# Computing the expert gates between the activation products of a PEER layer

## What is computed

```python
def peer(xn, w_q, sub_keys, u, v):
    ...
    best_s, best_pos = lax.top_k(cand_s, PEER_TOPK)
    idx = jnp.take_along_axis(cand_i, best_pos, axis=-1)
    gate = jax.nn.softmax(best_s, axis=-1)
    ...
        act = jnp.einsum("cd,ced->ce", xc, uc).astype(jnp.float32)
        hid = (jax.nn.gelu(act, approximate=False) * gc).astype(xc.dtype)
        return jnp.einsum("ce,ced->cd", hid, v[ic])
```

## Time and profile before

| | us |
|---|---|
| median of 3 runs (1920.65 to 1923.58) | 1921.12 |
| the profiled execution | 1920.95 |
| its span, from first to last instruction | 1919.2 |
| PE busy | 1662.7 (87%) |
| PE weight loads | 1331.6 (69%) |
| DVE busy | 1301.7 (68%) |
| ACT busy | 706.9 (37%) |
| POOL busy | 451.9 (24%) |

### The profile page before, as it was taken

How to read it: one execution, slowest core, us unless ns; L and a number is a source line. 1 busy time by engine, 2 the same in 40 slices (tenths; PEclk the granted TensorE clock), 3 DMA queues, 4 the chain that set the end, 5 groups by cost and what they waited for, 6 DMA issues and landing times. The chain is left out here.

```text
span 1919.2 us, 25753 instructions
## 1 busy us (share of the span) xinstructions
PE 1662.7 (87%) x9316; PEld 1331.6 (69%) x9316; DVE 1301.7 (68%) x1434; ACT 706.9 (37%) x929; POOL 451.9 (24%) x257
## 2 busy tenths in 40 slices
PE   6986998788887877788989959999996679999997
PEld 6855555444444536677678959999995568888886
DVE  3345887777777734855216996666659988888887
ACT  4514776666666624243233422222237720000000
POOL 5602111111111105532135840000019930000000
PEclk9996899999999988797999989999999989999999
DMA  8416999999999985421412533555550015555554
GB/s 282 144 50 259 367 397 397 396 396 396 396 396 397 397 324 149 173 89 47 158 37 111 176 131 132 185 187 178 192 176 0 0 66 197 195 188 189 194 196 142
DMA packets 142119, 406.90 MB, mean 212 GB/s; under 512 B 11128, under 2 KB 14328, under 8 KB 125560
## 3 DMA queue, kind: packets, MB, share of 16 engines
q1 hardware_dynamic: 136408, 395.77, 57.3%
q10 hardware_dynamic: 5664, 10.49, 1.5%
HBM read 396.80 MB, written 10.35 MB: 212 GB/s over the span
## 5 line engine op out<-in xcount | busy, mean ns | idle before, releaser
L1983 DVE TENSOR_TENSOR ring_rest<-ring,w_lead 128x2048 fp32r<-128x2048 f32 x128 | 291.7, 2320 | 86.1 <-ACT w_lead L1110 86.0
L1110 ACT ACTIVATE w_lead<-ring 128x2048 fp32r<-128x2048 f32 x128 | 237.8, 1904 | 92.2 <-DMA ring<-in_w_gate 42.9
L2187 DVE TENSOR_TENSOR rest<-raw,lead 128x2048 fp32r<-128x2048 f32 x112 | 256.8, 2293 | 3.9
L2179 DVE CAST lead<-raw 128x2048 fp32r<-128x2048 f32 x112 | 137.4, 1227 | 153.3 <-PE bank L1710 98.9
L711 POOL TENSOR_TENSOR ring_rest<-ring,half_lead 128x2048 fp32r<-128x2048 f32 (+1 forms) x38 | 172.5, 4554 | 233.6 <-ACT half_lead L705 233.5
L1513 PE MATMUL bank<-w_lead,x_two 128*128 128x512 f32 x512 | 154.6, 438 | 56.2 <-ACT w_lead L1110 49.1
L616 ACT ACTIVATE xhat<-h 128x1024 f32<-128x1024 f32 x6 | 6.3, 1056 | 457.0 <-DVE h L2254 360.7
L1513 PE MATMUL bank<-ring_rest,x_two 128*128 128x512 f32 x512 | 149.0, 419 | 29.3 <-DVE ring_rest L1983 29.1
L1513 PEld LDWEIGHTS bank<-w_lead,x_two 128*128 128x128 f32 x512 | 93.7, 200 | 115.8 <-ACT w_lead L1110 87.3
L1766 PE MATMUL bank<-lead,hid_hi 128*128 128x512 f32 x512 | 158.8, 392 | 5.5 <-DVE hid_lo L2230 5.5
L1766 PE MATMUL bank<-rest,hid_hi 128*128 128x512 f32 x512 | 158.6, 391 | 0.0
(11 more groups left out here) (317 smaller groups left out, 2710.5 us busy)
## 6 DMA issues: line engine op xcount, KB each, us to landing
ring<-in_w_gate SPq DMA_DIRECT2D x32, 2048.0 KB, 19.7
ring<-in_w_up SPq DMA_DIRECT2D x32, 2048.0 KB, 22.6
ring<-in_w_down SPq DMA_DIRECT2D x32, 2048.0 KB, 20.2
raw<-in_u SPq DMA_DIRECT2D x64, 1024.0 KB, 4.9
raw<-in_v SPq DMA_DIRECT2D x64, 1024.0 KB, 4.9
ring<-in_w_in SPq DMA_DIRECT2D x14, 2048.0 KB, 11.8
ring<-in_w_out SPq DMA_DIRECT2D x4, 2048.0 KB, 7.8
y_sorted<-y_blk ACTq DMA_DIRECT2D x64, 128.0 KB, 5.4
```

Of the source, the lines that this page charges most:

```text
L1110: act.activation(w_lead[half][:, :, :], ring8(slot)[:, 4 * half:4 * half + 4, :], ACT.Copy).then_inc(w_lead_ready, 1)
L1983: dve.tensor_tensor(ring_rest8(slot)[:, part, :], ring8(slot)[:, part, :], w_lead[half][:, :, :].bitcast(F32), ALU.subtract).then_inc(w_re ...
L2179: return dve.tensor_copy(dst, src)
L2187: dve.tensor_tensor(rest[slot][:, :], raw[slot][:, :], lead[b][:, :].bitcast(F32), ALU.subtract).then_inc(rest_ready, 1)
```

## The change

The gates' groups move from their own stage into the second part of the activation products. `ROUTING` goes from 16 to 24, so POOL and ACT split 24 chunks (POOL 25) before PE waits for the routing. From chunk 24 on the code of all engines is unrolled. `groups_in(n)` spreads the 64 groups over the 38 chunks 25 to 62: 26 of these have two groups, 12 have one. PE does a chunk's first half, the groups of that chunk, and then its second half. ACT makes `lead` for all chunks of `u`, its Gelu and its one-hots; DVE makes only `rest` there. DVE no longer multiplies a whole column in one go: where a token's gates come before the chunk's activation, DVE has copied the gates into `A` (`gate_columns`, the copy), ACT takes Gelu in place in PSUM, and `mix_columns` multiplies the two; where the activation came first, `gate_columns` multiplies as before. Activation products use three banks instead of two, gates three instead of four. POOL multiplies straight by `bestT` and no longer copies. Because `lead` is in use all the time, two of the three one-hot buffers lie on the residual `h`; SP saves `h` to DRAM before the stage and loads it back when all groups are done, and loads the last gain there too. Before the output products, the second chunk of `v` is split behind the last `mix_columns`. A semaphore is dropped elsewhere, its wait going to another with the same meaning.

```diff
-ROUTING = 16
+ROUTING = 24
+POOL_RESTS = ROUTING + 1
 PEER_CHUNKS = NKEYS // CJ
 HK = PEER_HEADS * TOPK
 GT = 4
 GROUPS = T // GT
-HOTS = 4
-VECTOR_HOTS = 1
-SCALAR_HOTS = HOTS - VECTOR_HOTS
+HOTS = 3
+FIRST_MIXED = POOL_RESTS
+LAST_MIXED = PEER_CHUNKS - 2
+def groups_through(n):
+    spans = LAST_MIXED - FIRST_MIXED + 1
+    return min(max(n - FIRST_MIXED + 1, 0), spans) * GROUPS // spans
+def groups_in(n):
+    return range(groups_through(n - 1), groups_through(n))
+def vector_makes_both(g):
+    return g % 4 == 0
+SCALAR_TURN = {g: k for k, g in enumerate(g for g in range(GROUPS) if not vector_makes_both(g))}
...
+        bestT = at("bestT", [P, T], WORK + 5120)
+        ijT = at("ijT", [P, 2, T], WORK + 6144)
+        hot = [at(f"hot{b}", [P, 2, GT, NKEYS], (H_AT, H_AT + 4096, WORK)[b]) for b in range(HOTS)]
+        h_kept = nc.dram_tensor("h_kept", (P, NT * D), F32, kind="Internal").ap()
...
+        ACT_BANK = [4, 5, 6]
+        GATE_BANK = [7, 0, 1]
+        ROUTE_BANK = [0, 1]
...
+            sp.dma_start(h_kept, h[:, :, :].rearrange("p t d -> p (t d)")).then_inc(h_saved, 16)
...
+            sp.wait_ge(gates_done, GROUPS)
+            sp.wait_ge(h_saved, 16)
+            sp.dma_start(h[:, :, :].rearrange("p t d -> p (t d)"), h_kept).then_inc(final_in, 16)
+            sp.wait_ge(chunk_used, PEER_CHUNKS)
+            sp.dma_start(gain_f[:, :], dram["norm_f_g"].broadcast_to([P, D])).then_inc(final_in, 16)
...
+            for n in range(ROUTING, POOL_RESTS):
+                pool_rest(n, n)
...
+            for g in range(GROUPS):
+                weighted = hot[g % HOTS][:, 1, :, :]
                 pool.wait_ge(hot_ready, g + 1)
...
-                pool.tensor_tensor(hot[b][:, 1, :, :], hot[b][:, 1, :, :],
-                                   spread(cur_g[:, b, :].unsqueeze(2), [P, GT, NKEYS]), ALU.mult).then_inc(hot_j_ready, 1)
...
+                pool.tensor_tensor(weighted, weighted, spread(bestT[:, g * GT:(g + 1) * GT].unsqueeze(2), [P, GT, NKEYS]),
+                                   ALU.mult).then_inc(hot_j_ready, 1)
...
+            def act_mixed_column(n):
+                done = GT * groups_through(n)
+                act.wait_ge(chunk_used, n + 1)
+                pair = pair_of(n)
+                if done < T:
+                    last = act.activation(A[:, n * CJ:(n + 1) * CJ, done:], pair[:, :, done:], ACT.Gelu)
+                if done:
+                    last = act.activation(pair[:, :, 0:done], pair[:, :, 0:done], ACT.Gelu)
+                last.then_inc(act_ready, 1)
+            def scalar_hot(g):
+                b, k = g % HOTS, SCALAR_TURN[g]
+                if g >= HOTS:
+                    act.wait_ge(gates_done, g - HOTS + 1)
...
+            for n in range(ROUTING - 1, PEER_CHUNKS):
+                if n + 1 < PEER_CHUNKS:
+                    act.wait_ge(chunk_used, n)
+                    act_lead(n + 1, n + 1, fill(0, n + 1))
+                act_mixed_column(n - 1)
+                if n + 1 == FIRST_MIXED:
+                    act.wait_ge(h_saved, 16)
+                    act.wait_ge(route_ready, 1)
+                for g in groups_in(n + 1):
+                    if not vector_makes_both(g):
+                        scalar_hot(g)
+            act_mixed_column(PEER_CHUNKS - 1)
...
+            def act_half_chunk(n, at_n, j):
                 slot, b = at_n % RAW_SLOTS, at_n % 2
-                bank_free(n, peeled)
                 hi = columns_of(lead[b], "u")
                 lo = columns_of(rest[slot], "u")
-                pe.wait_ge(lead_ready, n + 1)
-                for j in range(CJ):
-                    dst = bank[4 + b][:, j * T:(j + 1) * T]
-                    for x in (nT_hi, nT_lo):
-                        for k in range(KD):
-                            pe.matmul(dst, hi[:, k, j, :], x[:, k, :], start=(x is nT_hi and k == 0), stop=False)
-                    if j == 0:
-                        pe.wait_ge(rest_ready, n + 1)
+                dst = bank[ACT_BANK[at_n % 3]][:, j * T:(j + 1) * T]
+                if j == 0:
+                    pe.wait_ge(lead_ready, n + 1)
+                for x in (nT_hi, nT_lo):
                     for k in range(KD):
-                        last = pe.matmul(dst, lo[:, k, j, :], nT_hi[:, k, :], start=False, stop=(k == KD - 1))
-                last.then_inc(chunk_used, 1)
+                        pe.matmul(dst, hi[:, k, j, :], x[:, k, :], start=(x is nT_hi and k == 0), stop=False)
+                if j == 0:
+                    pe.wait_ge(rest_ready, n + 1)
+                for k in range(KD):
+                    last = pe.matmul(dst, lo[:, k, j, :], nT_hi[:, k, :], start=False, stop=(k == KD - 1))
+                return last
+            def act_chunk(n, at_n, peeled=False):
+                if not peeled or n >= 3:
+                    pe.wait_ge(act_ready, n - 2)
+                act_half_chunk(n, at_n, 0)
+                act_half_chunk(n, at_n, 1).then_inc(chunk_used, 1)
...
+            def gate_products(g):
+                b = g % HOTS
                 pe.wait_ge(hot_j_ready, g + 1)
-                if b >= VECTOR_HOTS:
-                    pe.wait_ge(hot_i_step, 2 * (SCALAR_HOTS * turn + b - VECTOR_HOTS) + 2)
-                if not peeled:
+                if not vector_makes_both(g):
+                    pe.wait_ge(hot_i_step, 2 * SCALAR_TURN[g] + 2)
+                if g >= HOTS:
                     pe.wait_ge(gated, g - HOTS + 1)
                 for t in range(GT):
-                    last = pe.matmul(bank[4 + b][:, t * NKEYS:(t + 1) * NKEYS], hot[b][:, 0, t, :], hot[b][:, 1, t, :],
+                    last = pe.matmul(bank[GATE_BANK[b]][:, t * NKEYS:(t + 1) * NKEYS], hot[b][:, 0, t, :], hot[b][:, 1, t, :],
                                      start=True, stop=True)
                 last.then_inc(gates_done, 1)
-            pe.wait_ge(route_ready, 1)
-            pe.wait_ge(act_ready, PEER_CHUNKS)
-            for b in range(HOTS):
-                gate_products(0, b, True)
-            with pe.Fori(1, GROUPS // HOTS) as turn:
-                for b in range(HOTS):
-                    gate_products(turn, b, False)
+            for n in range(ROUTING, PEER_CHUNKS):
+                if n - 3 < FIRST_MIXED:
+                    pe.wait_ge(act_ready, n - 2)
+                else:
+                    pe.wait_ge(columns_mixed, n - 3 - FIRST_MIXED + 1)
+                act_half_chunk(n, n, 0)
+                for g in groups_in(n):
+                    gate_products(g)
+                act_half_chunk(n, n, 1).then_inc(chunk_used, 1)
...
+            def rest_of(n):
+                slot, b = n % RAW_SLOTS, n % 2
+                dve.wait_ge(lead_ready, n + 1)
+                dve.tensor_tensor(rest[slot][:, :], raw[slot][:, :], lead[b][:, :].bitcast(F32), ALU.subtract).then_inc(rest_ready, 1)
+            def one_hots(g):
+                b = g % HOTS
+                first = 0 if vector_makes_both(g) else 1
                 whole = [P, 2 - first, GT, NKEYS]
+                if g >= HOTS:
+                    dve.wait_ge(gates_done, g - HOTS + 1)
                 dve.tensor_tensor(hot[b][:, first:, :, :], spread(c("iota")[:, 0:NKEYS].unsqueeze(1).unsqueeze(1), whole),
+                                  spread(ijT[:, first:, g * GT:(g + 1) * GT].unsqueeze(3), whole),
                                   ALU.is_equal).then_inc(hot_ready, 1)
+            def gate_columns(g, n):
                 dve.wait_ge(gates_done, g + 1)
+                if n > FIRST_MIXED:
+                    dve.wait_ge(columns_mixed, n - FIRST_MIXED)
+                gates = bank[GATE_BANK[g % HOTS]][:, :].rearrange("p (t j) -> p j t", t=GT)
+                tok = slice(g * GT, (g + 1) * GT)
+                ready = CJ * n
+                dve.tensor_copy(A[:, ready:, tok], gates[:, ready:, :])
+                dve.tensor_tensor(A[:, 0:ready, tok], gates[:, 0:ready, :], A[:, 0:ready, tok], ALU.mult).then_inc(gated, 1)
+            def mix_columns(n):
+                done = GT * groups_through(n)
+                dve.wait_ge(act_ready, n + 1)
+                dve.wait_ge(gated, groups_through(n))
+                view = A[:, n * CJ:(n + 1) * CJ, 0:done]
+                dve.tensor_tensor(view, pair_of(n)[:, :, 0:done], view, ALU.mult).then_inc(columns_mixed, 1)
+            dve.wait_ge(h_saved, 16)
             dve.wait_ge(route_ready, 1)
+            for g in groups_in(FIRST_MIXED):
+                one_hots(g)
+            dve.wait_ge(rest_ready, POOL_RESTS)
+            rest_of(POOL_RESTS)
+            for n in range(FIRST_MIXED, PEER_CHUNKS):
+                if n + 1 < PEER_CHUNKS:
+                    rest_of(n + 1)
+                if n > FIRST_MIXED:
+                    mix_columns(n - 1)
+                else:
+                    dve.wait_ge(act_ready, n)
+                for g in groups_in(n):
+                    gate_columns(g, n)
+                for g in groups_in(n + 1):
+                    one_hots(g)
...
```

(68 more changed lines are left out.)

54 lines of the change are left out of this document (12 added, 42 removed).

## The result

The changed kernel takes 1833.22 us (median of 4 runs, 1829.25 to 1833.95), the kernel before in the same sessions 1920.88. The ratio is 0.954 with a 95% interval of 0.952 to 0.956. Forecast were 1843.6 us with a range of 1829 to 1873, so the direction and the range held. Between the two profiled spans the gain is 87.3 us, forecast as 77.4. The narrower range given to the forecast itself, 1835 to 1856, was missed by 2 us, and the time is the one that rival (b) named.

The account below looks back on a forecast made before the run. The prediction took PE's own work and gaps as the bound. From 1920.95 us it summed - 16.1 - 64.3 - 2.6 + 0.6 + 1.0 + 4.0 = - 77.4, so 1843.6 us, own range 1835 to 1856, wider range 1829 to 1873.

Parts of the forecast that it names:

- rival (b): Mixed stage and routing: no collision and hardly any exclusion beside the routing, 4 and 7 us less, 1833; chance 0.12.
- collisions of DVE and POOL: Chunks with gates: 0.4 us lost in each of some ten chunks with two groups, 4 us in all.
- half clock, second chunk, gain ahead of chunk 66: Turn to output products: 2.6 us gained from the clock, 0.6 lost on `v`'s second chunk, 1 lost on the load.
- What bounds: Whole PEER layer: only what shortens PE's own row of work, or its gaps, counts.
- Part 1: Eight more chunks beside the routing, slowed by POOL and DVE excluding each other: chunk 24 begins 16.1 us earlier.
- Part 2, the price: Gates between the chunk halves: 0.95 us of PE a group, 60.8 in place of 125.1, gain 64.3 us.
- Part 2, whether it fits: Other engines beside PE in mixed chunks: fits on the mean, 20.6 against 21.9 us; some late chunks, 4 us.
- Part 3: Turn to output products and DMAs: 2.6 us gained without half clock, 0.6 and 1 us lost.
- (a): Mixed stage: DVE and POOL set the pace, DVE's `rest` ahead of POOL's second product; 31 us, 1871; chance 0.2.
- (c): Mixed stage: PE's short waits for groups keep it at the lower clock, kernel at some 2120; chance 0.04.
- (d): Mixed stage: no overlap, each group's chain stays on PE's path; only part 1 and the turn win, 1902; chance 0.04.

Follow-up runs that it names:

- e4: Changed kernel with the matmuls of every group done twice; 1891.9 us in one run, the mixed stage 342.7 us against 285.5.
- e2: Changed kernel with ROUTING 18 instead of 24, so the groups spread over 44 chunks instead of 38; 1844.1 us.
- e5: Changed kernel with ACT copying `raw` in place of POOL's `rest` for chunks 14 to 24, low part left out; 1826.6 us.
- e10: Changed kernel with digits and match matrix of DVE's routing in PSUM, in quarters of 512 elements; 1825.1 us, ratio 0.952.
- e3: Changed kernel with DVE making both one-hots of every group instead of every fourth; 1858.3 us, ratio 0.968.
- e7: Changed kernel with one more DVE operation of 512 elements, two SBUF inputs, for each group; 1845.1 us, ratio 0.962.
- e12: e3, and besides DVE begins `rest` only when POOL is done with the products of the groups just made; 1841.9 us, ratio 0.960.
- e1: Kernel before with ROUTING 22 instead of 16 and nothing else, gates in their own stage; 1901.9 us, ratio 0.991.

## Why the prediction was right, and 10 us too careful

| term | forecast | measured |
|---|---|---|
| chunk 24 begins earlier by | 16.1 | 18.7 |
| 64 groups in place of the gates stage | 60.8 for 125.1 | 57.0, and 0.3 to the first output product |
| collisions of DVE and POOL | 4.0 | 0 |
| half clock, second chunk, gain ahead of chunk 66 | gain 1.0 | gain 0.9 |
| span | - 77.4 | - 87.3 |

By these, 18.7 + 125.1 - 57.3 + 0.9 is 87.4.

**What bounds.** Right. PE has no gap in the mixed stage, e4's 57 us of added PE work came through whole, and e2's thinner spreading changed nothing.

**Part 1.** The mechanism was right in every piece: POOL's `rest` and DVE's two-SBUF-input operations took turns, PE paid, the routing was through before PE asked for it. e5 and e10 show the cause, and e10 that the input's place decides. The size: the chunks took 6.62 us, not the 6.9 that I played out, and six were slow as forecast. I gave every POOL wait 2.2 to 2.6 and halved it. The wait was 1.9 (6.50 instead of 4.63), and about half of that is the 0.91 that a chunk lost. The 1.9 was on the rows, 3.85 for two, and chunk 15 of the kernel before already took 6.6 us. My 6.9 is also the sum of the two full durations, 4.63 and 2.29; the turns are a little shorter:

```profile
1143.59 6.49 POOL L1008 TENSOR_TENSOR rest<-raw,lead 128x2048 fp32r<-128x2048 f32 x1
...
1145.63 6.59 DVE L2202 TENSOR_TENSOR match<-match,tif 128x2048 f32<-128x2048 f32 x1
...
1150.19 6.50 POOL L1008 TENSOR_TENSOR rest<-raw,lead 128x2048 fp32r<-128x2048 f32 x1
```

POOL ends at 1150.08, DVE 2.14 later at 1152.22, and POOL again 4.47 later at 1156.69: 6.6 for both turns, and that is a chunk. The size is worth 1.6 us. The transposes took 0.6, not 1.6: the 1.6 was measured on a PE at half clock after a stand (granted 0.50 from 1153 to 1155), and with the wait gone its price went too, 1.0 us. 18.7 is 1185.90 - 1035.08 against 1204.6 - 1035.1.

**Part 2, the price.** 0.89 instead of 0.95 a group, 3.8 us. (1471.3 - 1185.9) - 40 x 5.71 is 57.0; e4 gives 0.894. I had equated two kinds of eights since they last equally long; the duration of a record is not its distance to the next. The 81 ns of the Trainium skill's page (TensorE: Matmul & The Clock Gate, Back-to-back issue gap) would be 0.65 a group; e4 shows 0.112 us a record here, so that figure doesn't hold for these fp32 matmuls, as the prediction had it.

**Part 2, whether it fits.** The step that failed is the 4 us for late chunks with a group of DVE's own. PE waited for no group at all. I compared the sum of all exclusive work in one chunk (8.2) with PE's 7.6, but a chunk that is late by 0.6 is not one in which PE waits: PE wants the second product at 3.8 us of the chunk, and in the time line of the changed kernel POOL's pair is through 0.9 to 2.0 us before that. The right measure is the slack at that point and the order of DVE's `rest` and POOL's second product. e3, e7 and e12 show both: half a microsecond more in each one-hot turns the order and costs 25 us, 0.7 us more elsewhere costs 13, and a wait that restores the order gives 13 back. (The working's 7.45 and 5.05 are also 0.1 above their terms, 5.27 + 2.08 and 3.91 + 1.04, and its 11.3 for two chunks is 0.2 above 2.5 + 4.63 + 4.0; neither moves the forecast.)

**Part 3.** Right to 0.1 us in sum, and that is luck, since rest lies between 359.1 and 361.6 in the runs that don't touch it, and at 360.0 in e1 with the old turn. PE came to the output products at full clock, 0.31 us behind chunk 63. The first output chunk took 5.83 us instead of 8.17: 2.3 won, where 2.6 less 0.6 were forecast. The second took 6.71 instead of 5.44, with PE's wait of 1.0 for chunk 66 at its end: 1.3 lost, where 1.0 was forecast. That wait varied from 0 to 1.1 between the runs.

**The rivals.** (a) was not the case, but near: half a microsecond in each one-hot makes e3 of it. (b) named the measured time, 1833, for half the right reason: no collision, but the exclusion beside the routing was there, and the price of a group made up for it. Its number is luck. (c) had nothing for it: PE's clock was granted at 1.0 throughout, and in e3 too, where PE waited 13 times for up to 1.9 us. (d) fell with PE's closed row.

## What to carry to other kernels

When work moves into the cover of a busy engine, price it there by doubling it (e4), not by its records' durations; and ask of the covering engines not how busy they are but when the busy engine wants each piece, and what of theirs gets ahead of it. If two engines exclude each other, one mend is to put one input elsewhere (e10: 8.3 us in the chunks it touches, for five unused banks), another a wait that keeps the long operation behind the short one (e12: 13 us). Prices that were read behind a stand (a half clock, a cold start) go away with the stand.

## What the runs showed of the hardware

- VectorE's operations with two SBUF inputs and GpSimd's `rest` took turns: GpSimd's 4.63 us became 6.5 and VectorE's 2.29 became 4.3 and 6.59, each ending 4.5 or 2.1 us behind the other's end. With one of VectorE's inputs in PSUM both kept their times (e10).
- Two inputs aren't the condition in every case. A VectorE copy of 16 elements from SBUF to SBUF, 0.17 us in the kernel before with GpSimd idle, took 2.15 in the changed kernel and 2.87 in e10, and ended 0.03 us behind GpSimd's `rest` both times; the reduction out of SBUF kept its 2.29 beside GpSimd.
- The two engines settled into a beat here: chunks 15 to 21 had the same 6.62 us each, and PE the same 0.65 us wait.
- Eight fp32 matmul records of 128 columns cost 0.89 us in a stream, eight of 256 columns in fp32r 0.95, though both show durations of 1.1 us.
- Behind PE's wait of 2.3 us in e1 two eights show 1.9 us at a granted clock of 0.50, the lower of its two levels, before the pace was full again; beside the waits of 0.65 us, one in each 6.6 us, the granted clock stayed 1.00 from 1134 to 1188.
